# Router logits of a mixture-of-experts layer computed as two 64-column products, and one ScalarE table load moved ahead of the experts

## The chip, the cores and the metric

The kernel runs on one core of a Trainium2 chip. The metric is the device time of one execution in microseconds (us). Five engines run their own instruction streams and meet on semaphores: TensorE (matrix products), VectorE, ScalarE, GpSimd and SyncE (here it only issues transfers).

## The reference, cut to what matters

Two decoder layers over 512 tokens of width 1024; each has a mixer and then a hierarchical mixture of experts. What the change touches is the router and the start of the experts:

```python
def hierarchical_moe(h, wc, bc, wf, bf, w_gate_up, w_down):
    ...
    coarse_prob = jax.nn.softmax((xt @ wc + bc).astype(jnp.float32), axis=-1)   # 4 groups
    g_prob, g_idx = lax.top_k(coarse_prob, 1)
    fine_logits = (xt @ wf + bf).astype(jnp.float32).reshape(n, N_GROUPS, EXPERTS_PER_GROUP)
    ...
    e_logit, e_idx = lax.top_k(fine_sel, TOP_K_INNER)
    e_w = jax.nn.softmax(e_logit, axis=-1) * g_prob
    ...
    gate, up = jnp.split(gu, 2, axis=-1)
    act = jax.nn.silu(gate) * up * gates.astype(h.dtype)[..., None]
    return jnp.einsum('nef,efd->nd', act, w_down).reshape(b, t, d)
```

The kernel joins wc and wf into one matrix of 20 columns per layer.

## The kernel before

**Tiles.** The 512 tokens are 4 tiles of 128 (T = 0 to 3). TensorE computes `out = stationary^T @ moving`: the stationary operand is loaded by an LDWEIGHTS record, the moving one streamed by a MATMUL record. Dense products split each fp32 operand into a rounded high and a low part and are three products (L650, L651, L652, in helper `mm3`). The logits are plain fp32 products: one `mm` call shows as two LDWEIGHTS and two MATMUL records (64 calls over both layers, 128 records of L2023).

**The end of a mixer.** `outnorm(l, db)` on TensorE finishes the output projection tile by tile (`finish`, L650 to L652), turns the new x over (`rawT`, L1999, four transposes) and computes the logits of tiles whose halves are turned (`logits`, L2023): stationary is a 128x128 block of the turned x, moving is a 128x20 block of the router matrix, summed over eight blocks k. TensorE takes its instructions in the order written: finish(0), finish(1), rawT(0), finish(2), logits(0), rawT(1), half of finish(3), logits(1), rawT(2), the other half of finish(3), the first half of logits(3) and all of logits(2), rawT(3), the second half of logits(3). The eight calls of logits(0) are 16 records, likewise logits(1); then come 24 records in one burst, and 8 at the end.

VectorE adds each finished tile into x (L1429), copies the last turned tile out of the accumulator memory (L1451), multiplies it by the norm weight (L1452), and then runs `route(l)`, from L1736 on: some 35 small instructions in one chain that choose group and experts and build one-hot matrices. TensorE counts positions with them (L2399 to L2391); VectorE makes the rows of each expert's slots (L1780); GpSimd gathers the first two experts' tokens (L846). TensorE meanwhile multiplies for no result (`warm`, L2383), then turns the gathered tokens (L2377) and starts the experts: per expert 24 x 3 matrix products (L650 to L652), two transposes (L2447) of the activated values, and the down projection.

**ScalarE.** In `moe(l)` it takes two exponentials for the gates' weights (L1200, L1202; L1200 brings the table of Exp), then waits for the turned tokens (L1278), rounds weights (`hi`, L978 and L1227), and computes silu of the first expert's gate (L1207), which brings the table of Silu. VectorE multiplies silu by up and by the gate (L1841), behind making the low part of a weight piece (`lo`, L1836), in its own order. Copies work with whichever table is in place.

**Transfers.** SyncE streams the expert weights. Pieces from the thirteenth of a layer on wait until the first two experts' tokens have been gathered.

The logits lie in two banks of the accumulator memory, 40 columns of each: `logits_at = ps[:, 0:2, 0:40].rearrange("p b (t c) -> p t b c", t=2)`. `half(n)` is the partitions 64n to 64n+63; CH is 64, P is 128, KD is 8. `onec` is a column of ones. `A(...)` issues on ScalarE and waits for that instruction's end.

Of the kernel before, what the change touches and what calls it, by code (L numbers as in the profile page):

```python
# [26 lines left out]
ACT = mybir.ActivationFunctionType  # L27
AX = mybir.AxisListType

P = 128  # L30
# [3 lines left out]
KD = DM // P  # L34
NH = 4
DK = 128
CH = 64
# [282 lines left out]
def build(nc, a, out):  # L320
    ctx = ExitStack()
    with ctx:
        def sb(name, shape, dt=F32):
            return ctx.enter_context(nc.sbuf_tensor(name, shape, dt))

        def sem(name):
            return ctx.enter_context(nc.semaphore(name))
# [17 lines left out]
        small = sb("small", [P, 420])  # L345
# [14 lines left out]
        def reg(off, n):  # L360
            return ar[:, off:off + n]
# [5 lines left out]
        def v3(ap, k):  # L367
            return ap.rearrange("p (k n) -> p k n", k=k)
# [6 lines left out]
        onec = small[:, 412:413]  # L375
# [72 lines left out]
        def half(n):  # L448

            return slice(64 * n, 64 * n + 64)  # L450
# [25 lines left out]
        hTf = v3(reg(0, 4096), 8)  # L476
# [15 lines left out]
        def s_(name):  # L492
            if name not in SEM:
                SEM[name] = sem(name)
            return SEM[name]
# [149 lines left out]
        def cols(T, w=P):  # L645
            return slice(T * w, T * w + w)
# [43 lines left out]
        rw = v3(reg(RO + 1206, 160), 8)  # L690
# [10 lines left out]
        logits_at = ps[:, 0:2, 0:40].rearrange("p b (t c) -> p t b c", t=2)  # L701
# [267 lines left out]
        def _(act):  # L969
            A = Line(act, "act")  # L970
# [72 lines left out]
            def load_wb(n):  # L1043
                act.dma_start(wb(n), NORM_W[n].rearrange("(a n) -> a n", a=1).broadcast_to([P, DM])).then_inc(s_("wb_loaded"), 16)
# [151 lines left out]
            def moe(l):  # L1196
                m = MOE_PIECE[l]

                act.wait_ge(s_("r_cexp"), l + 1)
                A(act.activation(r_a, cd, ACT.Exp), s_("r_exp"))  # L1200
                act.wait_ge(s_("r_eexp"), l + 1)
                A(act.activation(ed, ed, ACT.Exp), s_("r_exp"))  # L1202
                used = s_("moe_used")

                def silu(E, par, count):
                    act.wait_ge(used, count)
                    act.activation(sg[:, par, :], ps[:, par, 0:FE], ACT.Silu).then_inc(s_("silu_done"), 1)  # L1207

                xT_hi(l, 0, 0)
                hi(m + 4)  # L1210
                hi(m + 5)
                xT_hi(l, 1, 1)
                hi(m + 6)
                silu(16 * l, 0, 6 * NE * l + 4)
                load_wb(2 * l + 2)

                def expert(it, par):
                    E = it * 2 + (16 * l + par)
                    b = m + 4 + 6 * par
                    last = isinstance(it, int) and it == NE // 2 - 1  # L1220

                    def hi_in(j):

                        n = b + j
                        act.wait_ge(raw_loaded[RAW_SLOTS[in_turn(n, it)]], raw_loaded_at(n, it))
                        act.wait_ge(used, it * 12 + (6 * NE * l + n - m - NSPL + 1))
                        act.activation(wh[:, n % NSPL, :, :], raw_at(in_turn(n, it)), ACT.Copy).then_inc(hi_done, 1)  # L1227

                    act.wait_ge(s_("aT_ready"), E + 1)
                    act.activation(HTH[:, 4 + par, 0:256], ps[:, 6, 0:256], ACT.Copy).then_inc(s_("aT_hi"), 1)  # L1230
                    n0 = 0
                    if not last or par == 0:
                        n0 = 4
                        for j in (3, 4, 5, 6):
                            hi_in(j)
                        silu(E + 1, 1 - par, it * 12 + (6 * NE * l + 6 * par + 8))
                        if not last:
                            xT_hi(l, it * 2 + (par + 2), par)
                        hi_in(7)
                    act.wait_ge(s_("ysb_free"), E + 1)  # L1240
                    for hf in range(2):
                        act.wait_ge(used, it * 12 + (6 * NE * l + 6 * par + 4 + n0 + hf + 1))
                        act.activation(ysb[:, par, 512 * hf:512 * hf + 512], ps[:, 2 + hf, :], ACT.Copy).then_inc(s_("y_read"), 1)
                        if hf == 0 and not last:
                            hi_in(8)

                for n in range(4):
                    expert(*divmod(n, 2))
                with act.Fori(2, NE // 2 - 1) as it:
                    for par in range(2):  # L1250
                        expert(it, par)
                for par in range(2):
                    expert(NE // 2 - 1, par)
                for i in range(4):
                    hi(m + 6 * NE + i)
                n = overflow_flag(act, l)
                with act.If(n > 0):
                    with act.Fori(0, 7) as j:
                        for g in range(2):
                            act.wait_ge(s_(f"ov_xT{l}"), j * 2 + (g + 1))  # L1260
                            act.activation(hTf[:, 4 * g:4 * g + 4, 0:P], v3(ps[:, 4 + g, :], 4), ACT.Copy).then_inc(s_(f"ov_xTr{l}"), 1)
                        act.wait_ge(s_(f"ov_gu{l}"), j + 1)
                        act.activation(sg[:, 0, :], ps[:, 0, 0:FE], ACT.Silu).then_inc(s_(f"ov_silu{l}"), 1)
                        act.wait_ge(s_(f"ov_aT{l}"), j + 1)
                        act.activation(hTf[:, 0:2, P:2 * P], ps[:, 6, 0:256].rearrange("p (k n) -> p k n", k=2), ACT.Copy).then_inc(s_(f"ov_aTr{l}"), 1)
                        for hf in range(2):
                            act.wait_ge(s_(f"ov_yp{l}"), j * 2 + (hf + 1))
                            act.activation(ysb[:, 0, 512 * hf:512 * hf + 512], ps[:, 2 + hf, :], ACT.Copy).then_inc(s_(f"ov_y{l}"), 1)

                act.wait_ge(s_("y_all_stored"), l + 1)  # L1270
                src = y2_dram[l].rearrange("(T p j) d -> T p j d", p=P, j=2)
                for T in range(NT):
                    act.dma_start(YP[:, T, :, :], src[T]).then_inc(s_(f"yp_loaded{T}"), 16)
# [8 lines left out]
            for step in SCHEDULE:  # L1282
                k = step[0]
# [674 lines left out]
        def _(pe):  # L1958
            mm = nc.tensor.matmul
# [42 lines left out]
            def outnorm(l, db):  # L2002
                def finish(t, kps=(2, 3)):
                    for kp in kps:
                        i = first_piece(db) + kp
                        if t == 0:
                            pe.wait_ge(hi_done, i + 1)
                            wait_lo(pe, i)
                        for k2 in range(2):
                            k = 2 * kp + k2  # L2010
                            ins = mm3(ps[:, t, :], HTH[:, k, cols(t)], HTL[:, k, cols(t)], wh[:, i % NSPL, k2, :], wl[:, i % NSPL, k2, :],
                                      False, k == KD - 1)
                        if t == NT - 1 and kp == 2:
                            ins.then_inc(piece_used, 1)
                    if kp == 3:
                        ins.then_inc(dense_ready, 1)

                def logits(T, halves_of_row=(0, 1)):
                    for hf in halves_of_row:
                        if hf == 1:  # L2020
                            tile_is_read(pe, ("xT", l, 1, T))
                        for k in range(4 * hf, 4 * hf + 4):
                            ins = mm(logits_at[:, T // 2, T % 2, :], hTf[:, k, cols(T)], rw[:, k, :], start=k == 0, stop=k == KD - 1)  # L2023
                    if T == NT - 1 and halves_of_row[-1] == 1:
                        ins.then_inc(s_("r_logits"), 1)

                finish(0)
                finish(1)
                rawT(l, 1, 0)
                finish(2)  # L2030
                tile_is_read(pe, ("xT", l, 0, NT - 1))
                pe.wait_ge(s_("norm_w_applied"), 2 * l + 1)
                logits(0)
                rawT(l, 1, 1)
                finish(3, (2,))
                logits(1)
                rawT(l, 1, 2)
                finish(3, (3,))
                logits(3, (0,))
                logits(2)  # L2040
                rawT(l, 1, 3)
                logits(3, (1,))
# [455 lines left out]
            for hf in range(2):  # L2498
                ins = mm(ps[:, hf, :], one_row, wrow[:, 512 * hf:512 * hf + 512], start=True, stop=True)
            ins.then_inc(s_("wb0_spread"), 1)  # L2500
            for step in SCHEDULE:
                k = step[0]
# [118 lines left out]
```

## Time and profile before

| what | value |
|---|---|
| median of 3 runs | 1235.07 us (1231.03, 1235.31, 1235.07) |
| the profiled execution, its own time | 1230.59 us |
| its span in the profile | 1228.5 us |
| TensorE busy with products | 1115.8 us, 91% of the span |
| VectorE busy | 684.2 us, 56% |
| ScalarE busy | 597.0 us, 49% |
| GpSimd busy | 421.9 us, 34% |

All stages and durations below are of the profiled execution, whose time is its span and 2.1 us around it. Layer 0's router lies at about 397 to 427 us, layer 1's at about 1011 to 1041 us. In the rows, PE is TensorE's products, PEld its weight loads, DVE VectorE, ACT ScalarE, POOL GpSimd, SP SyncE.

### The profile page before, as it was taken

The page shows a single profiled execution, that of the slowest core. Times are in us where ns is not written, and L with a number is a line of the kernel's source. Part 1 is how long each engine was busy: PE and PEld are TensorE (multiplying, and loading weights), DVE is VectorE, ACT ScalarE, POOL GpSimd, SP SyncE. Part 2 cuts the span into 40 slices and gives each one's busy share as a digit, 9 for nine tenths or more (in the row PEclk, how much of TensorE's full clock was granted, in tenths as well). Part 3 has the DMA queues.
Part 4 walks back from the last instruction along what each step waited for, and adds up shares of the span by engine and source line. Part 5 has one row for each costly group of instructions (what it writes and reads, how often), then busy time and mean ns, then how long its engine had stood idle before and what let it go on. Part 6 is the DMA issues. An engine that isn't in the chain of part 4 may idle for free.

```text
span 1228.5 us, 19674 instructions
## 1 busy us (share of the span) xinstructions
PE 1115.8 (91%) x7081; PEld 918.3 (75%) x7081; DVE 684.2 (56%) x973; ACT 597.0 (49%) x873; POOL 421.9 (34%) x350
## 2 busy tenths in 40 slices
PE   6998999999979799998399999999999997999980
PEld 4786888778758578886378888888888885788870
DVE  3434424358633699997614532542433136999975
ACT  4546233251423389998232324333253233899871
POOL 4342311210205134444434243542434431344442
PEclk8999999999989799999599999999999997999995
DMA  9232211102206399997633232232212262999955
GB/s 250 57 86 52 54 53 36 53 32 74 69 1 201 114 362 371 378 375 257 242 96 102 78 94 70 86 105 76 94 63 93 86 197 98 359 375 366 365 205 214
DMA packets 89285, 194.75 MB, mean 159 GB/s; under 512 B 20158, under 2 KB 21242, under 8 KB 88187
## 3 DMA queue, kind: packets, MB, share of 16 engines
q1 hardware_dynamic: 67562, 159.87, 39.0%
q10 hardware_dynamic: 11856, 17.07, 4.0%
q0 software_dynamic: 9792, 16.80, 3.7%
q8 instruction: 49, 0.80, 0.3%
q14 instruction: 26, 0.21, 0.1%
HBM read 189.50 MB, written 23.07 MB: 173 GB/s over the span
## 4 chain that ended last, share of the span: by engine, by line
PE 82%; DVE 8%; ACT 3%; DMA 3%; issue 2%; SPq 1%; POOL 1%; POOLq 0%; DVEq 0%; ACTq 0%
PE ps L650 23%; PE ps L651 22%; PE ps L652 22%; PE ps L2377 2%; PE ps L2169 2%; DMA raw<-in_moe_w_down_dram 1%; PE ps L2023 1%; PE ps L2383 1%; DMA arena<-y 1%; PE ps L2307 1%; PE ps L2055 1%; DVE arena L1410 1%; DVE x L1391 1%; DVE x L1392 1%; DMA x<-in_x_dram 1%
## 5 line engine op out<-in xcount | busy, mean ns | idle before, releaser
L814 POOL TENSOR_TENSOR wl<-raw,wh 128x1024 fp32r<-128x1024 f32 x100 | 243.1, 2439 | 423.1 <-ACT wh L978 422.7
L650 PE MATMUL ps<-wh,hT_hi 128*128 128x512 f32 x864 | 349.7, 405 | 13.3 <-DVE hT_lo L1461 6.0
L652 PE MATMUL ps<-wh,hT_lo 128*128 128x512 f32 x864 | 340.0, 393 | 0.0
L651 PE MATMUL ps<-wl,hT_hi 128*128 128x512 f32 x864 | 339.8, 393 | 0.0
L978 ACT ACTIVATE wh<-raw 128x1024 fp32r<-128x1024 f32 x116 | 122.7, 1068 | 221.9 <-PE ps L652 203.2
L650 PEld LDWEIGHTS ps<-wh,hT_hi 128*128 128x128 f32 x864 | 164.3, 190 | 49.2 <-DVE hT_lo L1461 6.9
L652 PEld LDWEIGHTS ps<-wh,hT_lo 128*128 128x128 f32 x864 | 163.9, 190 | 35.2
L651 PEld LDWEIGHTS ps<-wl,hT_hi 128*128 128x128 f32 x864 | 164.4, 190 | 31.2
L650 PE MATMUL ps<-hT_hi,wh 128*128 128x512 f32 x288 | 117.4, 407 | 8.2 <-ACT arena L1136 5.3
L1836 DVE TENSOR_TENSOR wl<-arena,wh 128x1024 fp32r<-128x1024 f32 x96 | 114.0, 1222 | 5.5 <-ACT wh L1227 3.9
L1836 DVE TENSOR_TENSOR wl<-raw,wh 128x1024 fp32r<-128x1024 f32 x92 | 109.5, 1224 | 11.6 <-ACT wh L978 4.8
L651 PE MATMUL ps<-hT_lo,wh 128*128 128x512 f32 x288 | 114.8, 399 | 0.0
L652 PE MATMUL ps<-hT_hi,wl 128*128 128x512 f32 x288 | 114.3, 397 | 0.0
L1227 ACT ACTIVATE wh<-arena 128x1024 fp32r<-128x1024 f32 x94 | 98.8, 1070 | 8.9 <-PE ps L652 6.1
L1227 ACT ACTIVATE wh<-raw 128x1024 fp32r<-128x1024 f32 x84 | 88.1, 1072 | 7.3 <-PE ps L652 3.3
L650 PEld LDWEIGHTS ps<-hT_hi,wh 128*128 128x128 f32 x288 | 55.4, 192 | 22.8 <-issue 4.3
L652 PEld LDWEIGHTS ps<-hT_hi,wl 128*128 128x128 f32 x288 | 55.6, 193 | 12.1
L651 PEld LDWEIGHTS ps<-hT_lo,wh 128*128 128x128 f32 x288 | 55.7, 193 | 11.0
L859 POOL COPY cur_rows<-slot_rows 128x1 uint32 (+1 forms) x32 | 8.5, 267 | 134.7 <-PE ps L2377 134.7
L825 POOL TENSOR_TENSOR small<-small 128x4 f32<-128x4 f32 (+1 forms) x10 | 13.9, 1394 | 100.7 <-DVE small L1580 100.7
L992 ACT ACTIVATE arena<-x 128x1024 f32<-128x1024 f32 x20 | 21.2, 1058 | 52.1 <-DVE x L1392 36.8
L1278 ACT ACTIVATE hT_hi<-ps 128x512 fp32r<-128x512 f32 x64 | 34.7, 595 | 20.3 <-PE ps L2377 18.9
(317 smaller groups left out, 1561.8 us busy)
## 6 DMA issues: line engine op xcount, KB each, us to landing
raw<-in_moe_w_gate_up_dram SPq DMA_DIRECT2D x64, 512.0 KB
arena<-in_moe_w_gate_up_dram SPq DMA_DIRECT2D x64, 512.0 KB, 6.7
raw<-in_odd_w_in_dram SPq DMA_DIRECT2D x48, 512.0 KB
raw<-in_even_w_in_dram SPq DMA_DIRECT2D x32, 512.0 KB
arena<-in_moe_w_down_dram SPq DMA_DIRECT2D x32, 512.0 KB, 7.8
raw<-in_moe_w_down_dram SPq DMA_DIRECT2D x32, 512.0 KB
arena<-y ACTq DMA_DIRECT2D x8, 1024.0 KB, 8.2
raw<-in_odd_w_out_dram SPq DMA_DIRECT2D x16, 512.0 KB
```

What stands on the lines that cost most here:

```text
L650: nc.tensor.matmul(dst, lh, rh, start=first, stop=False)
L651: nc.tensor.matmul(dst, lh, rl, start=False, stop=False)
L652: return nc.tensor.matmul(dst, ll, rh, start=False, stop=last)
L814: pool.tensor_tensor(columns_of(i, wl[:, i % NSPL, :, :]), raw_columns(i), columns_of(i, wh[:, i % NSPL, :, :]).bitcast(F32), ALU.subtract ...
L825: pool.tensor_tensor(dst, src, mhalf[:, 0:n], ALU.pow).then_inc(on, 1)
L978: act.activation(columns_of(i, wh[:, i % NSPL, :, :]), raw_columns(i), ACT.Copy).then_inc(hi_done, 1)
L992: A(act.activation(squares(n), X[:, T, :], ACT.Square, scale=DM ** -0.5, accum_out=ss[:, T:T + 1]), s_("norm_ss"))
L1227: act.activation(wh[:, n % NSPL, :, :], raw_at(in_turn(n, it)), ACT.Copy).then_inc(hi_done, 1)
L1278: act.activation(HTH[:, 2 * par + g, :], ps[:, 4 + g, :], ACT.Copy).then_inc(s_("xT_hi"), 1)
L1836: tt(wl[:, n % NSPL, :, :], raw_at(in_turn(n, it)), wh[:, n % NSPL, :, :].bitcast(F32), ALU.subtract).then_inc(lo_dve, 1)
L2169: blocks(name, lambda o, b, n: mm(o, of_block(lh, b, n), of_block(rh, b, n), start=True, stop=True))
L2377: ins = tr(ps[:, 4 + g, cols(j)], xg[:, par, 4 * g + j:DM:KD], ident[:, :])
```

## The change

The logits of a tile are computed as two products of 64 tokens each, one into the upper and one into the lower 64 partitions of the same accumulator columns, alternating inside each k. And `moe(l)` gets one more ScalarE instruction behind the second exponential: silu of one value per partition into an unused column of `small`.

```diff
                 A(act.activation(r_a, cd, ACT.Exp), s_("r_exp"))
                 act.wait_ge(s_("r_eexp"), l + 1)
                 A(act.activation(ed, ed, ACT.Exp), s_("r_exp"))
+                A(act.activation(small[:, 413:414], onec, ACT.Silu))
                 used = s_("moe_used")
...
                         for k in range(4 * hf, 4 * hf + 4):
-                            ins = mm(logits_at[:, T // 2, T % 2, :], hTf[:, k, cols(T)], rw[:, k, :], start=k == 0, stop=k == KD - 1)
+                            for n in range(2):
+                                o = P * T + CH * n
+                                ins = mm(logits_at[half(n), T // 2, T % 2, :], hTf[:, k, o:o + CH], rw[:, k, :], start=k == 0, stop=k == KD - 1)
                     if T == NT - 1 and halves_of_row[-1] == 1:
                         ins.then_inc(s_("r_logits"), 1)
```

## Rows read from the trace of the kernel before

**Rows 1.** The page: the chain that ended last, by line.

```profile
PE ps L650 23%; PE ps L651 22%; PE ps L652 22%; PE ps L2377 2%; PE ps L2169 2%; DMA raw<-in_moe_w_down_dram 1%; PE ps L2023 1%; PE ps L2383 1%; DMA arena<-y 1%; PE ps L2307 1%; PE ps L2055 1%; DVE arena L1410 1%; DVE x L1391 1%; DVE x L1392 1%; DMA x<-in_x_dram 1%
```

**Rows 2.** Stretches: length, busy us and records of engines, TensorE clock, DMA share, GB/s.

```profile
397.00:410.00 13.00, 12.15 (x92) 11.14 (x90) 5.87 (x7) 3.56 (x7) 2.38 (x6) 1.00 0.46 185
...
440.00:480.00 40.00, 40.00 (x201) 33.65 (x200) 38.89 (x43) 36.56 (x52) 17.20 (x24) 1.00 0.96 364
```

**Rows 3.** Timeline, layer 0, TensorE: start, length, instruction, idle time before it.

```profile
397.50 0.40 PE L652 MATMUL ps<-wh,hT_lo 128*128 128x512 f32 x1
...
397.73 1.86 PE L2023 MATMUL ps<-arena 128*128 128x20 f32 x16
...
399.44 0.63 PE L1999 MATMUL ps<-ident,x 128*128 128x128 f32 x4
...
404.85 2.75 PE L2023 MATMUL ps<-arena 128*128 128x20 f32 x24
...
407.44 0.64 PE L1999 MATMUL ps<-ident,x 128*128 128x128 f32 x4
```

**Rows 4.** Timeline, layer 0, the hand-over from the logits to the router.

```profile
405.12 0.69 DVE L1429 TENSOR_TENSOR x<-x,ps 128x512 f32<-128x512 f32 x1 [2.90 <-PE ps L652]
...
408.18 0.69 DVE L1451 COPY arena<-ps 128x512 f32<-128x512 f32 x1 [2.38 <-PE ps L1999]
408.91 1.22 DVE L1452 TENSOR_TENSOR arena<-x,arena 128x1024 f32<-128x1024 f32 x1
...
410.17 0.24 DVE L1736 TENSOR_TENSOR arena<-ps,small 128x80 f32<-128x80 f32 x1
```

**Rows 5.** Timeline, layer 1, the same hand-over.

```profile
1022.33 1.22 DVE L1452 TENSOR_TENSOR arena<-x,arena 128x1024 f32<-128x1024 f32 x1
1022.35 1.90 PE L2023 MATMUL ps<-arena 128*128 128x20 f32 x8 [0.85 <-DVE arena L1451]
...
1024.38 0.24 DVE L1736 TENSOR_TENSOR arena<-ps,small 128x80 f32<-128x80 f32 x1 [0.83 <-PE ps L2023]
```

**Rows 6.** Timeline, TensorE, a burst of 32 records with 64-column stationary blocks.

```profile
124.19 0.39 PE L652 MATMUL ps<-hT_hi,wl 128*128 128x512 f32 x1
124.51 1.15 PE L2182 MATMUL ps<-arena 128*64 128x64 f32 x32
125.59 0.50 PE L650 MATMUL ps<-hT_hi,wh 128*128 128x512 f32 x1
125.93 0.40 PE L651 MATMUL ps<-hT_lo,wh 128*128 128x512 f32 x1
```

**Rows 7.** Timeline, TensorE, a burst of 64 such records, and what follows it.

```profile
288.07 2.06 PE L2307 MATMUL ps<-arena 128*64 128x32 f32 x64
290.06 0.50 PE L650 MATMUL ps<-wh,hT_hi 128*128 128x512 f32 x1
```

**Rows 8.** Timeline, layer 0, the first expert's gate.

```profile
433.27 0.39 PE L652 MATMUL ps<-wh,hT_lo 128*128 128x512 f32 x1
433.48 1.28 ACT L1207 ACT_TABLE_LOAD   x1
...
433.54 1.21 DVE L1836 TENSOR_TENSOR wl<-arena,wh 128x1024 fp32r<-128x1024 f32 x1
...
435.19 0.42 DVE L1841 TENSOR_TENSOR arena<-arena,ps 128x256 f32<-128x256 f32 x1 [0.43 <-ACT arena L1207]
```

**Rows 9.** Timeline, layer 0, ScalarE between the second exponential and its next work.

```profile
415.36 0.20 ACT L1202 ACTIVATE arena<-arena 128x4 f32<-128x4 f32 x1
...
425.03 1.09 ACT L1278 ACTIVATE hT_hi<-ps 128x512 fp32r<-128x512 f32 x2 [9.47 <-PE ps L2377]
```

**Rows 10.** Stretches around layer 1's last logits, columns as in rows 2.

```profile
1006.00:1021.00 15.00, 15.00 (x103) 13.59 (x102) 5.99 (x7) 6.39 (x11) 3.73 (x9) 1.00 0.31 128
1021.00:1025.00 4.00, 2.39 (x12) 1.94 (x10) 2.47 (x5) 1.15 (x1) 0.30 (x1) 0.52 0.32 131
```

**Rows 11.** SyncE's wait before the stream of a layer's expert weights.

```profile
SPq L748 <- DMA arena<-hs,slot_rows: 33.9, 1, 33.9
```

## The prediction

> **What bounds the kernel now.** Start with the page's chain that ended last [rows 1]: the three dense-product lines alone are 67% of it, and the logits' line L2023 is 1%, some 12 us over two layers. So the change can only work on a small part, and its worth has to be read from the stretch where that part lies. The stretches show that TensorE works 12.15 of 13.00 us around the logits of layer 0 [rows 2]: what shortens TensorE's order there moves everything behind it. The timeline of the stretch says what ends it: VectorE's L1429 idles for a product, L1451 idles for the last transposes (L1999), L1452 follows, and the router's L1736 starts only when L1452 is through [rows 4]. From L1736 on, VectorE's chain sets the time, not TensorE. In layer 1 the last wait is another one: L1452 ends at 1022.33 + 1.22 = 1023.55, and L1736 waits 0.83 us more for the last eight logits records [rows 5].
>
> **Part one: the logits in halves.** A call shows as two records, so the 16 records of a tile become 32, the burst of 24 becomes 48 and the last 8 become 16. The work per record is what I must price from elsewhere, since no 64-column logits are in this trace.
>
> Before: from the start of a 16-record burst to the start of the transposes behind it is 399.44 - 397.73 = 1.71 us, and 407.44 - 404.85 = 2.59 for the 24 [rows 3]: 0.107 us a record. That is not the streaming of 20 columns; it is the pace at which full 128-column blocks are loaded and used.
>
> After: the nearest rows are bursts that alternate between the lower and the upper 64 output partitions, as the change does, with 64 or 32 moving columns. From burst start to the next product's start, 32 records take 125.59 - 124.51 = 1.08 us [rows 6] and 64 take 290.06 - 288.07 = 1.99 [rows 7]. The difference, 0.91 us for 32 records, is 0.028 a record, and 1.08 - 0.91 = 0.17 is a fixed part. Entering and leaving costs more: the burst begins 0.32 us behind the product before it, the full-width logits begin 0.23 behind theirs (397.50 to 397.73) [rows 3], which adds 0.09. The first product after the burst takes 0.34 to the next one (125.59 to 125.93), 0.11 over that pace; full-width bursts lose something behind them too, so I count 0.03 of it, a choice, and keep the other 0.08 for the range. So I take 0.12 for the change of shape beside the 0.17 in the burst.
>
> - A 16-record burst: 1.08 + 0.12 = 1.20 in place of 1.71, a gain of 0.51. There are two before the last finish, 1.02.
> - The burst of 24: 1.08 + 16 x 0.028 + 0.12 = 1.65 in place of 2.59, a gain of 0.94.
> - The last 8: 8 x 0.107 = 0.86 becomes 1.08 - 16 x 0.028 = 0.63 plus 0.12, a gain of 0.11. In layer 0 it is worth nothing: it begins with L1452 and is over before L1452 ends after 1.22 us, and would be up to 0.1 without that cover.
>
> Does something else become late before the transposes? Tile 3's x must be added first: L1429 takes 0.69 us from 405.12 [rows 4], and moves 1.02 earlier with the last finish, to 404.10 to 404.79. TensorE would be ready for the last transposes at 407.44 - 1.96 = 405.48. TensorE still decides, by 0.7 us. So L1451, L1452 and L1736 all come 1.02 + 0.94 = 1.96 us earlier in layer 0.
>
> In layer 1 the same 1.96 us come off, and the extra wait of 0.83 can go too. There TensorE's granted clock was 1.00 from 1006 to 1021 and 0.52 on average from 1021 to 1025 [rows 10], that is mostly the 1.2 GHz level; the last eight records took 1.90 us in place of some 0.86 to 1.1. TensorE had gone through the 24-record burst just before the clock fell. At the lower level, with everything doubled, the 16 half-width records would take about 1.26 + 0.12 = 1.38 us, 0.2 past L1452; at the upper one they hide wholly. Bounds of this term: 0 (other executions may not have the fall there) and 0.83. I take 0.7, nearer to the row of this execution.
>
> Behind L1736 the whole train moves: the router's chain, the gather, the warm-up products, the experts. The weight stream is the thing that might stay behind, for in the experts' stage DMA is at 0.96 of its share and 364 GB/s [rows 2]. But SyncE waited 33.9 us for the gathered tokens before it went on with the stream [rows 11], so the stream starts earlier with the router. GpSimd has nothing in its queue before that gather that the change would touch.
>
> A rule speaks against the halves. The nearest rows change shape twice at a price of 0.09 to 0.12 us, already in the sum. The Trainium skill says in "TensorEngine Tiling (Array Packing)", Key Properties, that a change of tiling mode drains TensorE; it names no price, so by that rule too each of the eight bursts pays, and the sum stays as the rows make it; the trace agrees, with 0.32 us in place of 0.23 at the entrance [rows 6].
>
> **Part two: the table.** The new instruction adds one table load (1.28 us, the duration of L1207's own [rows 8]) and one small activation (0.20, as L1202) on ScalarE, behind 415.56. ScalarE then sat idle 9.47 us before L1278 [rows 9], so these 1.48 us are hidden; without that cover they would be on the path, 1.5 us a layer. Queued behind it are only the roundings of the turned tokens, which wait for TensorE anyway. The exponentials have signalled before it, so nobody else waits.
>
> At the other end L1207's load goes. It started at 433.48, and the last product of the gate began at 433.27 and took 0.39, to 433.66. So silu could start at about 433.7 in place of 434.77, ending at 434.1. But L1841, which uses it, stands behind L1836 on VectorE, which ends at 433.54 + 1.21 = 434.75 [rows 8]. Before, L1841 started at 435.19 after 0.43 idle. What is late next is thus L1836, and of 1.28 us only 0.43 come off. TensorE's next instructions in its order are the transposes of L1841's result, so the 0.43 are on the path, in layer 1 likewise (its table load has the same place there).
>
> **The sum.** Layer 0: 1.96 + 0.43 = 2.4. Layer 1: 1.96 + 0.7 + 0.43 = 3.1. Together 5.5 us off the profiled execution's 1230.59, giving 1225.1; off the median of 1235.07, 1229.6. The four executions known are 1230.59, 1231.03, 1235.07 and 1235.31: two levels some 4 us apart, equally often. The median happens to be of the upper pair, so a new median may fall in either. Between 1225.1 and 1229.6, leaning to the upper value, I forecast **1228.5 us**.
>
> **Rivals.**
>
> *The halves do not overlap (0.10).* Two 64-column blocks might cost what one of 128 does: 0.053 us a record. Then 32 records take 1.71 + 0.12, a loss of 0.12 a burst, 0.36 a layer before the router, and only the table's 0.86 remains: 1235.07 - 0.86 + 0.72 = 1234.9. The Trainium skill gives such a rule, in "TensorE: Matmul & The Clock Gate", Part 3, The mechanism: weight loads overlap with products in flight only when the row group differs; here it does not. Against this rival: the bursts of rows 6 and 7 have all 128 rows too, alternate in columns alone, and ran at 0.028.
>
> *Accumulation makes half-width records slow (0.05), slower than before.* The logits sum eight k into the same 20 columns; rows 6 and 7 do not sum over calls. If each record waited for its forerunner in the accumulator and kept the 0.107, 56 more records ahead of the last transposes would cost 6.0 us a layer, and the last burst 16 x 0.107 = 1.71 would outlast L1452 by 0.5. Both layers: 13.0 + 0.5 for shape changes - 0.86 = 12.6 more, 1247.7. It decides against the change from (1.71 - 0.29) / 32 = 0.044 us a record. Against it: the two records of one call already go to the same place in rows 6 and 7, and full-width logits run at the same 0.107 whatever they sum.
>
> *Gained, and given back (0.13).* The experts' stage runs into the weight stream, at 0.96 of DMA, or the clock rises later against the first experts' products, since the fall and rise need not move with the work. One layer's part of 2 to 3 us is lost: 1235.07 - 2.5 = 1232.6. For it: the two levels of the runs show that something of 4 us varies. Against it: the stream starts with the gather [rows 11].
>
> *My forecast (0.72).* Its own range is 1224 to 1231.5: sums from 4.8 (no clock term) to 5.6, each from either level, and a microsecond for the price of a shape change before transposes, which no row shows.
>
> **How the numbers follow.** A measurement of this kernel tells about 0.5% from nothing, that is 6.2 us: below 1228.9 is faster. The forecast's 0.72 splits by the level of the median: 0.50 faster, 0.22 the same. The given-back rival adds 0.03 faster and 0.10 same; no overlap adds 0.08 same and 0.02 slower; accumulation 0.05 slower. Faster 0.53, same 0.40, slower 0.07. The range 1223 to 1233 takes in the forecast's own and the given-back case, and leaves out the two others with 0.15.
>
> **What the profile after would show.** L2023 in 256 records at 128x64 blocks, each 16-record place at 1.1 us and the long one at 1.6; last transposes some 2 us nearer to the stretch's start; L1736 directly behind L1452 in both layers; a table load behind L1202 and none at L1207, with L1841 directly behind L1836. The prediction is wrong if the records come at over 0.04 us, if TensorE idles for L1429 or L1016's copies inside the bursts, if the gather does not move with L1780, or if TensorE waits in the experts where it did not before.

## The result, and the profile after

The changed kernel takes 1223.59 us (median of 6 runs, 1220.57 to 1227.23) against 1230.59 us for the kernel before in 6 runs (1229.73 to 1235.31): the ratio is 0.9939, with a 95% interval of 0.9917 to 0.9960. That is 7.0 us off by the medians, 7.5 by the ratio, with an interval of 4.9 to 10.2. The profiled execution took 1223.59 us, its span is 1221.4 us against 1228.5.

The kernel's line numbers move: L1451 of before is L1452 here, L1736 is L1737, L1841 is L1842, L1999 is L2000, L2023 is L2026, L2377 is L2380, L1207 is L1208.

The chain that ended last, from the page of the changed kernel. The logits, 1% of the chain before [rows 1], are no longer in what it lists:

```profile
span 1221.4 us, 19932 instructions
...
PE ps L650 23%; PE ps L652 22%; PE ps L651 22%; PE ps L2380 2%; PE ps L2172 2%; DMA raw<-in_moe_w_gate_up_dram 1%; DMA arena<-y 1%; DVE arena L1411 1%; PE ps L2310 1%; ACTq L1346 1%; PE ps L2058 1%; DVE x L1392 1%; DVE x L1393 1%; PE ps L2386 1%; PE ps L2135 1%
```

The bursts of layer 0 in the timeline of the changed kernel, to be read against [rows 3]:

```profile
396.17 1.11 PE L2026 MATMUL ps<-arena 128*64 128x20 f32 x32
...
397.22 0.66 PE L2000 MATMUL ps<-ident,x 128*128 128x128 f32 x4
...
401.89 0.39 PE L652 MATMUL ps<-wh,hT_lo 128*128 128x512 f32 x1
402.21 1.58 PE L2026 MATMUL ps<-arena 128*64 128x20 f32 x48
```

From the burst's start to the transposes it is 1.05 us in place of 1.71, and 1.51 (402.21 to 403.72) in place of 2.59. Entering costs 0.32 behind the product before it, 0.09 more than full width. A 32-record burst thus gains 0.57 and the long one 0.99, 2.13 us a layer.

The hand-over to the router in layer 0, and the same in layer 1, against [rows 4, 5]:

```profile
405.20 1.22 DVE L1453 TENSOR_TENSOR arena<-x,arena 128x1024 f32<-128x1024 f32 x1
405.23 0.65 PE L2026 MATMUL ps<-arena 128*64 128x20 f32 x16 [0.85 <-DVE arena L1452]
406.46 0.24 DVE L1737 TENSOR_TENSOR arena<-ps,small 128x80 f32<-128x80 f32 x1
...
1017.50 1.22 DVE L1453 TENSOR_TENSOR arena<-x,arena 128x1024 f32<-128x1024 f32 x1
1017.52 0.65 PE L2026 MATMUL ps<-arena 128*64 128x20 f32 x16 [0.85 <-DVE arena L1452]
1018.76 0.24 DVE L1737 TENSOR_TENSOR arena<-ps,small 128x80 f32<-128x80 f32 x1
```

In both layers the router now starts directly behind L1453. Layer 1's wait of 0.83 us is gone: the last logits took 0.65 us in place of 1.90. The two are not at the same clock: in the kernel before it had fallen to 0.50 when they ran, here it was still at 1.00 (from 1017.5 to 1018.2 us). At 1.00 the full-width ones took 1.07 us, in layer 0 of the kernel before, and caused no wait either.

The table, in the timeline of the changed kernel, against [rows 8, 9]. The load sits behind the second exponential; silu (L1208) starts as soon as its product is there; and the gate's product (L1842) now stands directly behind the weight piece (L1837):

```profile
411.65 0.20 ACT L1202 ACTIVATE arena<-arena 128x4 f32<-128x4 f32 x1
411.87 1.28 ACT L1203 ACT_TABLE_LOAD   x1
...
421.18 1.09 ACT L1279 ACTIVATE hT_hi<-ps 128x512 fp32r<-128x512 f32 x2 [7.81 <-PE ps L2380]
...
429.81 1.22 DVE L1837 TENSOR_TENSOR wl<-arena,wh 128x1024 fp32r<-128x1024 f32 x1
429.97 0.38 ACT L1208 ACTIVATE arena<-ps 128x256 f32<-128x256 f32 x1 [0.24 <-PE ps L652]
430.94 0.42 DVE L1842 TENSOR_TENSOR arena<-arena,ps 128x256 f32<-128x256 f32 x1
431.50 0.43 PE L2450 MATMUL ps<-ident,arena 128*128 128x128 f32 x2 [1.35 <-DVE arena L1842]
```

**Where the 7.1 us of the span came from.** The starts of the same instructions in the two profiles, and how far the changed kernel is ahead:

| place | before | after | ahead | gained since |
|---|---|---|---|---|
| layer 0, first logits | 397.73 | 396.17 | 1.56 | 1.56 |
| layer 0, router (L1736, L1737) | 410.17 | 406.46 | 3.71 | 2.15 |
| layer 0, first gate's product | 435.19 | 430.94 | 4.25 | 0.54 |
| layer 1, first logits | 1011.05 | 1008.47 | 2.58 | -1.67 |
| layer 1, router | 1024.38 | 1018.76 | 5.62 | 3.04 |
| end of the span | 1228.5 | 1221.4 | 7.1 | 1.5 |

The changed code cannot reach the first row's 1.56 us: they lie ahead of it. The changed kernel was 0.8 us ahead at 12 us of the span and 1.6 at 30, behind a stretch (12 to 30 us) whose clock was 0.72 before and 1.00 after. The 2.15, 0.54 and 3.04 lie where the change works, though 0.89 of the 3.04 also hangs on where the clock fell. Of the last row's 1.5, 0.5 is layer 1's share of the table load. The loss of 1.67 and the other 1.0 are the odd ones, and lie in the experts' stages. There TensorE goes from expert to expert in 9.35 us, until it meets late weights. (In the trace an expert is 12 x 3 products of L650 to L652, 8 x 3 for gate and up and 4 x 3 for down, not the 24 x 3 named ahead.) Waits among the changed kernel's experts, two of ScalarE's from 540 to 575 us and then one of TensorE's from 430 to 600 us (waiting line, awaited, us in total, times, longest):

```profile
ACT wh L1228 <- DMA raw<-in_moe_w_gate_up_dram: 1.6, 1, 1.6
ACT wh L1228 <- DMA arena<-in_moe_w_gate_up_dram: 1.4, 2, 1.0
```

```profile
PE ps L650 <- DVE hT_lo L1829: 1.1, 2, 0.9
```

In layer 0 the kernel before had only 0.2 us of ScalarE waiting for weights there, and no such wait of TensorE; it lost 2.0 us in layer 1. What this is, and why the moved load did more than the 0.43 us foretold for it, is what the experiments are about.

### The profile page after: what moved, and what is told of

It is laid out like the page before. It is cut to its first block, busy times and chain, and to the rows that moved or that the text cites. A ratio compares the mean times of both kernels' runs of the same rounds, so it can differ in the third digit from the quotient of the medians.

```text
span 1221.4 us, 19932 instructions
## 1 busy us (share of the span) xinstructions
PE 1109.1 (91%) x7209; PEld 909.9 (74%) x7209; DVE 687.5 (56%) x973; ACT 597.0 (49%) x875; POOL 423.2 (35%) x350
## 4 chain that ended last, share of the span: by engine, by line
PE 80%; DVE 9%; DMA 3%; ACT 3%; issue 2%; ACTq 1%; SPq 1%; POOL 1%; POOLq 0%; DVEq 0%
PE ps L650 23%; PE ps L652 22%; PE ps L651 22%; PE ps L2380 2%; PE ps L2172 2%; DMA raw<-in_moe_w_gate_up_dram 1%; DMA arena<-y 1%; DVE arena L1411 1%; PE ps L2310 1%; ACTq L1346 1%; PE ps L2058 1%; DVE x L1392 1%; DVE x L1393 1%; PE ps L2386 1%; PE ps L2135 1%
## 5 line engine op out<-in xcount | busy, mean ns | idle before, releaser
L650 PE MATMUL ps<-wh,hT_hi 128*128 128x512 f32 x864 | 349.0, 404 | 13.3 <-DVE hT_lo L1462 6.1
L652 PE MATMUL ps<-wh,hT_lo 128*128 128x512 f32 x864 | 339.9, 393 | 0.0
L650 PEld LDWEIGHTS ps<-wh,hT_hi 128*128 128x128 f32 x864 | 164.1, 190 | 49.4 <-DVE hT_lo L1462 7.0
L652 PEld LDWEIGHTS ps<-wh,hT_lo 128*128 128x128 f32 x864 | 163.5, 189 | 35.0
L650 PE MATMUL ps<-hT_hi,wh 128*128 128x512 f32 x288 | 117.5, 408 | 7.0 <-ACT arena L1136 4.1
L1837 DVE TENSOR_TENSOR wl<-arena,wh 128x1024 fp32r<-128x1024 f32 x96 | 114.0, 1223 | 5.4 <-ACT wh L1228 4.1
L1837 DVE TENSOR_TENSOR wl<-raw,wh 128x1024 fp32r<-128x1024 f32 x92 | 109.7, 1224 | 11.9 <-ACT wh L1228 5.1
L652 PE MATMUL ps<-hT_hi,wl 128*128 128x512 f32 x288 | 114.7, 398 | 0.0
L650 PEld LDWEIGHTS ps<-hT_hi,wh 128*128 128x128 f32 x288 | 55.7, 193 | 22.0 <-issue 4.3
L652 PEld LDWEIGHTS ps<-hT_hi,wl 128*128 128x128 f32 x288 | 55.6, 193 | 12.1
```

The lines of the kernel that those rows point to most:

```text
L650: nc.tensor.matmul(dst, lh, rh, start=first, stop=False)
L652: return nc.tensor.matmul(dst, ll, rh, start=False, stop=last)
L1837: tt(wl[:, n % NSPL, :, :], raw_at(in_turn(n, it)), wh[:, n % NSPL, :, :].bitcast(F32), ALU.subtract).then_inc(lo_dve, 1)
```

## The experiments

Each ran beside the kernel before on the same chip. The theories: (1) the halves give most, since the two halves' records overlap; (2) the moved load gives more than it takes off the path. The main rival to the second is that it gives just that. All times in us.

| kernel | median (runs) | ratio to before, 95% interval |
|---|---|---|
| changed kernel | 1223.59 (6) | 0.9939, 0.9917 to 0.9960 |
| e1 halves, load not moved | 1226.20 (7) | 0.9961, 0.9945 to 0.9976 |
| e2 load moved, full width | 1228.68 (12) | 0.9979, 0.9968 to 0.9990 |
| e3 halves in turn | 1225.48 (9) | 0.9962, 0.9948 to 0.9976 |
| e4 quarters | 1221.56 (4) | 0.9920, 0.9897 to 0.9943 |
| e5 halves, load not moved, gap filled | 1223.60 (6) | 0.9950, 0.9935 to 0.9965 |
| e6 a lighter weight stream | 1220.64 (4) | 0.9917, 0.9903 to 0.9931 |
| e7 gate's product first | 1223.41 (6) | 0.9939, 0.9925 to 0.9953 |
| e8 quarters, gate's product first | 1221.40 (6) | 0.9924, 0.9910 to 0.9938 |
| e9 before, gap filled | 1229.19 (12) | 0.9990, 0.9978 to 1.0002 |
| e11 quarters, gap filled | 1222.14 (6) | 0.9926, 0.9911 to 0.9941 |

The kernel before itself had medians of 1230.86 (23 runs, 1227.38 to 1233.34), 1231.01 (11) and 1230.91 (17, to 1235.03) beside them. e10 and e12 are single runs.

### e1: the halves alone, and e2: the moved load alone

```diff
 # e1
-                A(act.activation(small[:, 413:414], onec, ACT.Silu))
 # e2
-                            for n in range(2):
-                                o = P * T + CH * n
-                                ins = mm(logits_at[half(n), ...], hTf[:, k, o:o + CH], ...)
+                            ins = mm(logits_at[:, T // 2, T % 2, :], hTf[:, k, cols(T)], ...)
```

> The halves without the moved table load. Theory (most of the gain comes from the halves): the bursts of L2026 as in the changed kernel (1.1 us for 32 records, 1.6 for 48), the first gate's table load back at its old place with about 0.5 us more TensorE idle per layer; 5 to 6.5 us faster than before, that is 0.995 to 0.996 of its time. Rival (the table load is what gave most): under 2 us faster.

> The moved table load with the logits in full width. Theory: TensorE's gap before the first activated values' transposes shrinks from 2.0 to 1.5 us in each layer, so about 1.0 us faster than before, 0.999 of its time. Rival (a ScalarE load of 1.28 us off the path in each layer): 2.6 us faster, 0.998.

Measured: 1226.2 for the halves, 4.8 us off by the ratio, a little under the range; 1228.7 for the load, 2.6 off by the ratio, where 1.0 was expected. TensorE's gap shrank as said in e2, from 2.03 to 1.51 us between product starts in both layers. So the size matches the rival's, but not its mechanism. The trace of e1 has the answer. Its table load is at the old place, and here is what followed the gap in layer 0, in stretches (length, busy us and records of PE, PEld, DVE, ACT, POOL, then the granted clock, DMA share, GB/s):

```profile
431.00:434.00 3.00, 1.14 (x14) 0.68 (x13) 2.50 (x7) 2.12 (x3) 0.32 (x1) 1.00 1.03 379
434.00:435.00 1.00, 1.00 (x5) 0.81 (x4) 0.86 (x5) 0.79 (x2) 0.00 (x0) 0.79 1.04 422
435.00:436.00 1.00, 1.00 (x4) 0.77 (x3) 0.83 (x6) 0.54 (x1) 0.00 (x0) 0.50 1.01 406
436.00:438.00 2.00, 2.00 (x6) 1.54 (x5) 1.93 (x5) 1.06 (x1) 0.00 (x0) 0.50 1.03 390
```

TensorE was busy 1.14 of 3 us, and then, though busy all the time, at the 1.2 GHz level (0.50). The first products of the second expert took 0.63 us each in place of 0.39. The same in layer 1 of e1:

```profile
1049.00:1053.00 4.00, 4.00 (x12) 0.58 0.99 377
```

The same stretch of the changed kernel's layer 0, whose gap was 0.5 us shorter, stayed at 2.4 GHz:

```profile
432.00:436.00 4.00, 4.00 (x18) 3.29 (x18) 3.66 (x13) 3.43 (x4) 0.00 (x0) 1.00 1.02 379
```

The price can be read from the starts of the gate's product from expert to expert. Intervals of the first four experts:

```
changed kernel, layer 0      8.04  8.89  9.35
e1, layer 0                  9.19  9.35  9.35
e1, layer 1                  9.18  9.37  9.34
```

That is 1.6 us lost a layer. In this execution of e1 the load at its old place cost 0.5 + 1.6 us in each layer.

### e5: fill the gap instead of moving the load, and e9: fill it in the kernel before

```diff
                 slots_to_rows(over_at, hotO, ...).then_inc(s_("r_rows"), 1)
+                warm(6)     # six 128x512 products for no result
```

> The halves without the moved table load, and TensorE multiplies six more times for no result in the two idle microseconds ahead of the first activated values' transposes (1.4 of the 2.0 us filled). Theory (the 2.0 us of idle are followed by a stretch at the 1.2 GHz level, which costs the first experts about 1.6 us a layer; the moved load helps most by shortening that gap): no lower clock between the first and the third expert in either layer, and 2 to 3.5 us less than with the halves alone, that is 1223 to 1224.5. Rival (the moved load is worth what it takes off the path, 0.5 us a layer): the time of the halves alone, 1226, since the gap itself stays.

> The kernel before with the six filling products ahead of the first activated values' transposes, nothing else changed. Theory (the kernel before meets the 1.2 GHz level after its gap of 2.0 us in some executions and layers, which is why the moved load alone gained 2.2 us and not the 0.9 to 1.0 that it takes off the path): no lower clock there, and 1 to 2 us less than before, 1229 to 1230. Rival (the kernel before keeps its clock there always, as in its profile, and the moved load's 2.2 us have another source): within 0.5 us of before.

Measured: e5 has a median of 1223.60, inside its range, with the table load still on ScalarE's path. Its timeline shows the filling products (L2385) between the last group and the transposes, and a clock of 1.00 behind them in both layers:

```profile
430.62 1.62 PE L2385 MATMUL ps<-hT_hi 128*128 128x512 f32 x6
432.63 0.43 PE L2450 MATMUL ps<-ident,arena 128*128 128x128 f32 x2 [0.39 <-DVE arena L1841]
```

```profile
430.00:440.00 10.00, 9.61 (x55) 1.00 1.02 398
1040.00:1050.00 10.00, 9.61 (x55) 1.00 1.02 367
```

The median is that of the changed kernel, but the ratios put e5 between the two: 6.2 us off, against 4.8 for e1 and 7.5 for the changed kernel. That is what the account asks for, since the filling prevents the fall (1.6 us an execution on average, see below) and leaves the load's 2 x 0.5 us on the path. The ratios' intervals overlap, so this is carried by the trace (the intervals between gates are 8.05 and 8.85 us in e5), not by the timing alone. e9 came out at 1229.19, 1.2 us under before by the ratio and 1.7 by the medians, within its expectation, but with an interval that just reaches 1: this run by itself does not prove it. The 1.6 us expected on average lie within that interval.

### e10 and e12: how often does the clock fall there?

No edit: the kernel before, and e1, once more.

> The kernel before once more, for a second profile. Theory: either a stretch at 1.2 GHz behind the gap in at least one layer and second and third experts that are 0.5 to 1.1 us longer there, or the state of the first profile; a TensorE wait at experts 12 to 15 in one layer or both.

> The halves without the moved load once more, for a second profile. Theory (the fall behind the 2.0 us gap depends on where the gap lies in the chip's own time): the 1.2 GHz level follows the gap in none, one or both layers, and wherever it does, the first two intervals between experts' gates are 9.2 and 9.35 us, and elsewhere 8.05 and 8.9.

Measured: e10 took 1230.93 us and had the fall in layer 0, not in layer 1; e12 took 1225.64, and had it in layer 0 and not in layer 1, too. The stretches behind the gap, of e10 and then e12:

```profile
436.00:439.00 3.00, 3.00 (x9) 0.51 1.02 397
```

```profile
434.00:437.00 3.00, 3.00 (x8) 0.50 1.01 395
...
1035.00:1050.00 15.00, 12.44 (x69) 1.00 0.85 311
```

The intervals agree: 9.16 and 9.35 us in e10's layer 0 against 8.04 and 8.88 in its layer 1; 9.21 and 9.37 against 8.05 and 8.88 in e12. Over all profiles: with the gap of 2.0 us (before, e10, e1, e12) the lower clock followed in 4 of 8 layers. With the load moved (changed kernel, e2, e3, e4, e6, e7, e8, e11) in none of 16: ten of these with the gap of 1.5 us, four with 1.0 (e7, e8), two with it filled (e11). With the gap filled in the old place (e5, e9) it followed in none of 4. Four of eight is a rough share, and the cause of its coming and going is not shown. At one in two, moving the load saves 2 x 0.5 for the path and about 2 x 0.8 on average for the clock, 2.6 us. That is e2's 2.6, and the 2.6 between the medians of e1 and the changed kernel.

The profiles show a second fall that comes and goes: the one ahead of a layer's last eight logits records. Where the clock was 1.00 during them (layer 0 of before, layer 1 of e2), the router waited 0.03 to 0.04 us; at 0.63 (layer 0 of e10) 0.48; at 0.50 (the other five layers of the four profiles at full width) 0.82 to 0.83. With halves (changed kernel, e1, e3, e5, e6, e7, e12) the router waited in none of 14 layers. In most of them the fall came only after the burst, so that they do not test a burst at the lower clock. The nearest to a test is layer 1 of e5, where the mean clock was 0.55 over the 16 records:

```profile
1016.21 1.22 DVE L1452 TENSOR_TENSOR arena<-x,arena 128x1024 f32<-128x1024 f32 x1
1016.23 1.00 PE L2025 MATMUL ps<-arena 128*64 128x20 f32 x16 [0.85 <-DVE arena L1451]
...
1017.47 0.24 DVE L1736 TENSOR_TENSOR arena<-ps,small 128x80 f32<-128x80 f32 x1
```

They took 1.00 us and were still hidden behind L1452's 1.22.

### e3: halves in turn, and e4: quarters

```diff
 # e3: eight records of one half, then eight of the other
-                        for k in range(4 * hf, 4 * hf + 4):
-                            for n in range(2):
+                        for n in range(2):
+                            for k in range(4 * hf, 4 * hf + 4):
 # e4: four blocks of 32 tokens
-                            for n in range(2):
-                                o = P * T + CH * n
-                                ins = mm(logits_at[half(n), T // 2, T % 2, :], hTf[:, k, o:o + CH], ...)
+                            for n in range(4):
+                                o = P * T + 32 * n
+                                ins = mm(logits_at[32 * n:32 * n + 32, T // 2, T % 2, :], hTf[:, k, o:o + 32], ...)
```

> The same 64-column products, but four k of the lower half and then four k of the upper one, so that eight records in a row have the same half. Theory (what makes the halves cheap is that the weight load of one half runs beside the product in the other): the pace falls to about 0.053 us a record, 32 records take 1.8 to 2.0 us, as much as full width or more, and the gain on the whole shrinks to 0 to 2 us. Rival (a narrower block is cheaper by itself, whatever its neighbour is): 0.028 a record as in the changed kernel, and its whole gain of 7 us.

> The logits as four products of 32 tokens each, alternating over the four quarters. Theory (a record cannot be had under about 0.028 us, so that halves are the best width): a tile's 64 records take about 2.0 us, more than the 1.7 us of full width, and the burst of 96 about 2.9; the gain on the whole is gone, 1 to 3 us slower than before without the table's share. Rival (the pace is set by the columns loaded, so quarters take 0.014 us a record): a tile's 64 records take 1.1 us, the same time as the changed kernel or up to 0.3 us less a burst.

The first burst of e3's layer 0 and the transposes behind it:

```profile
397.10 1.42 PE L2026 MATMUL ps<-arena 128*64 128x20 f32 x32
398.45 0.65 PE L2000 MATMUL ps<-ident,x 128*128 128x128 f32 x4
```

1.35 us, between the changed kernel's 1.05 and full width's 1.71: neither 1.8 to 2.0 nor the rival's 1.05. The single records say why. In the changed kernel they start alternately 7 and 51 ns apart, a pair in 58: the two halves go side by side. (A record does not name its half; that is inferred from the program's order and from e3.) In e3 records with the same half before and behind them start 58 ns apart. But where one group of eight meets the next, most come 26 to 32 ns apart and one pair 6, closer than records of one half ever come alone. So the next half's records must have started beside the former's. The load records have the same rhythm (6 or 7 and 49 to 52 ns in the changed kernel), so loads of both halves run side by side too; whether load or product sets the 58 ns is not separated. So both statements of the theory hold for single records (a half by itself costs 58 ns, and the gain comes from the neighbour being the other half), and the sum made of them was wrong, since part of the overlap came about by itself. The whole took 1225.48, 1.9 more than the changed kernel, the 1.9 us that the slower bursts make over both layers (2 x 0.30 and 0.36 in each); the two ratios' intervals overlap, so the agreement is closer than the timing can show.

The first and the long burst of e4's layer 0, and their transposes:

```profile
395.13 0.74 PE L2026 MATMUL ps<-arena 128*32 128x20 f32 x64
395.81 0.66 PE L2000 MATMUL ps<-ident,x 128*128 128x128 f32 x4
...
400.43 1.01 PE L2026 MATMUL ps<-arena 128*32 128x20 f32 x96
401.43 0.63 PE L2000 MATMUL ps<-ident,x 128*128 128x128 f32 x4
```

64 records in 0.68 us, 96 in 1.00: 0.010 us a record. My theory of a floor of 0.028 a record is wrong. The rival was right that quarters are cheaper still, and with its 0.014 too careful. The kernel is 1221.56, 2.0 under the changed one, though the intervals of the two ratios overlap. Part of the bursts' 1.2 us a layer isn't had: the router now waits for something else, the last tile's scale from GpSimd. VectorE in layer 0 of e4:

```profile
402.89 1.23 DVE L1453 TENSOR_TENSOR arena<-x,arena 128x1024 f32<-128x1024 f32 x1
404.63 0.24 DVE L1737 TENSOR_TENSOR arena<-ps,small 128x80 f32<-128x80 f32 x1 [0.52 <-POOL small L830]
```

### e6: a lighter weight stream

From the thirteenth weight piece of a layer on, each piece that goes to one of the six plain buffers is loaded for half its columns; the experts' results use old values there.

```diff
-                sp.dma_start(raw_at(i), piece_src(i))...
+                dst, src = raw_at(i), piece_src(i)
+                if RAW_SLOTS[i] < NRAW and any(m + 12 <= i < m + 6 * NE for m in MOE_PIECE):
+                    dst, src = dst[:, :, 0:256], src[:, :, 0:256]
+                sp.dma_start(dst, src)...        # likewise in the loop
```

> The changed kernel, with every weight piece that goes to one of the six plain buffers loaded for half its columns only, from the thirteenth piece of a layer on, so that a quarter less is streamed in the experts' stage (the output uses old values in the other half). Theory (part of the gain in layer 0 was given back at experts 12 to 14, where TensorE ran into the weight stream): no TensorE wait there in either layer, an expert every 9.35 us from the third to the last, and 2 to 4 us less than the changed kernel, about 1220.5. Rival (what was lost there comes from something other than the stream, such as the gathers or GpSimd's order): the waits stay, and the time within 1 us of 1223.6.

Measured: 1220.64, 3.0 under the changed kernel, with another result of the computation. The same stretch of the late experts, first of the changed kernel, then of e6 (PE busy, clock, DMA share, GB/s):

```profile
540.00:560.00 20.00, 18.94 (x92) 1.00 1.00 355
```

```profile
540.00:560.00 20.00, 20.00 (x101) 1.00 0.71 248
```

The intervals between the last six gates of layer 0 are 9.46, 10.51, 10.51, 8.84, 9.04 in the changed kernel from the eleventh on, and 9.35 (9.34 to 9.41) in e6. Both layers of e6 are free of them, so the waits are from the stream. Against e6, the late experts (the tenth interval on) cost the kernel before 0.0 and 2.0 us in its two layers, the changed one 1.6 and 0.6, e5 0.0 and 1.5, e9 0.4 and 0.3, e1 0.9 and 0.0, e2 1.1 and 2.8, e3 2.5 and 1.8, e4 0.9 and 3.2, e7 0.4 and 1.8, e8 1.0 and 0.7, e10 0.0 and 1.0, e11 0.2 and 0.6, e12 0.5 and 0.9. So most of the 1.67 us lost in the table of the result is this wait, and the 1.0 gained is its opposite: 2.0 - 0.6 = 1.4 us, of which 0.4 went again behind the experts. The wait fell in another layer, and the two executions lost 2.0 and 2.2 in all. In this pair of profiles it is thus not the change's gain given back. On average that is open. The three profiles with logits and load as before lost 2.0, 1.0 and 0.7 us over both layers, 1.2 on average; the ten changed ones (e6 left out) lost 0.8 to 4.3, 2.3 on average. The spread is too wide for one profile a kernel to settle it, and the kernel before was not run with the lighter stream.

### e7 and e8: the gate's product ahead of the weight piece; e11: the gap filled as well

```diff
 # e7 (and e8, on top of the quarters), VectorE
-                lo_in(m + 6)
                 gated(16 * l, 0)
+                lo_in(m + 6)
 # e11, on top of the quarters, TensorE: warm(4) where e5 has warm(6)
```

> The changed kernel with two VectorE instructions of the first expert swapped: the gate's product ahead of the low part of weight piece 6. Theory (behind the moved load VectorE's weight piece is what holds the gate): TensorE's gap there shrinks from 1.5 to about 1.0 us in both layers, and 0.5 to 1.1 us come off the whole. Rival (the weight piece made later is missed by TensorE at once): the gap moves to the products of the second expert, no change.

> Logits in quarters, the moved table load, and the swap of the run before. Theory: the two add, 2 to 2.5 us from the quarters and up to 1 us from the swap below the changed kernel, so 1220 to 1221. Rival (what the router gains is given back to the weight stream): within 1 us of the changed kernel's 1223.6.

> Quarters, the moved load, and four filling products in the 1.5 us gap. Theory (with the moved load the gap is too short for the clock to fall anyway): no change from the quarters alone, 1221 to 1222. Rival (it still falls in some executions): 0.5 to 1.5 us less and a narrower spread.

e7: 1223.41 against 1223.59, no change; the rival was right. The gap fell from 1.51 to 0.96 us between product starts, and a new one of 1.07 came behind it: TensorE at once misses the weight piece that was put back. The waits of e7's TensorE from 425 to 445 us:

```profile
PE ps L2450 <- DVE arena L1842: 0.8, 1, 0.8
PE ps L650 <- DVE wl L1837: 0.7, 1, 0.7
```

e8 is 1221.40, as the quarters alone (1221.56). It lies within its range, but the swap adds nothing to it. e11 is 1222.14, also the same: with the load moved there is no fall left for the filling to prevent. The fastest version with the whole computation is thus the quarters with the moved load, 0.8% under before, in e4; of e4, e8 and e11 none is clearly ahead of another.

## Why the prediction was right, and where it was off

- **Halves.** Right in mechanism and size. Foretold were 1.96 us a layer; 2.13 came by the bursts, 2.15 by the shift of layer 0's router. A 32-record burst gained 0.57 where 0.51 was foretold, the long one 0.99 for 0.94: the bursts of 64-column blocks [rows 6, 7] were a good measure, a little dear. Summing over k costs nothing, so the rival of slow accumulation fell with the records' pace.
- **No overlap.** That rival fell as well. The rule of "TensorE: Matmul & The Clock Gate", Part 3, The mechanism, in the Trainium skill, that weight loads overlap products in flight only when the row group differs, does not hold as far as the whole pace goes: in the changed kernel all records have all rows and differ in columns only, and a pair of different halves started every 58 ns, as did a single record between two of the same half (e3).
- **Change of shape.** 0.09 us at the entrance as foretold; what the burst costs behind it was inside the 0.17 taken.
- **The last eight records' wait.** Foretold 0.7 for layer 1's 0.83; all of it went, 3.04 - 2.15 = 0.89 us with the rest. That was counted for one layer because the one profile had it in one. At full width six of eight layers had it, 4.7 us over four executions, so the term is worth 1.2 us on average. The price of the half-width records at the lower clock, 1.38 us and 0.2 past L1452, was too high as far as e5's 1.00 us at a mean clock of 0.55 tells.
- **Table load, what it frees.** 0.43 us a layer foretold; TensorE's gap shrank by 0.51, and L1842 stood behind L1837, as said. The load at its new place cost nothing: 7.81 us of idle time were left behind it.
- **Table load, what it prevents.** This was missed. The sum took the gap of 2.0 us as a wait that costs its own length. It also lets the clock fall in one layer of two, at 1.6 us each. The profile of before did not show it, since that execution was spared in both layers.
- **Behind the router.** That all moves with it is right: the lead won in layer 0 stayed constant to 0.03 us over its first eleven experts. "TensorE waits in the experts where it did not before" was named as a sign of being wrong, and it came, 1.6 us in layer 0. It proves less than was thought, since the kernel before has such waits too, in the other layer. The rival's 1232.6 did not come; whether a part of the gain is given back on average is open (see e6).
- **The sum, and the forecast.** 5.5 us of 1230.59, 1225.1, was the sum. Two terms were too small for an average execution: nothing in place of 1.6 us for the fall behind the gap, and 0.7 in place of 1.2 for the router's wait. With both it would have been 7.6, where 7.0 was measured by the medians; the interval of 4.9 to 10.2 us holds the 5.5 as well. The 1228.5 named was 4.9 us too high. The 1223.59 lies 0.6 us inside the range of 1223 to 1233 and just below the forecast's own 1224 to 1231.5, so it was a near thing. The mechanisms held, and the step that failed is the one from the sum to the median: "two levels some 4 us apart, equally often", leaning to the upper one. The runs of the kernel before beside the experiments spread over 1227.4 to 1235.0, with medians of 1230.9 to 1231.0. They do not fall into two levels; three runs had given a high median, and a drop from the profiled execution's own time was the better forecast. That execution lay in the middle.

## What to carry to other kernels

Products with few moving columns and a 128-column stationary block can be bound by the stationary block. Here their pace went with its width, and 64-column blocks came as pairs every 58 ns with 20 moving columns as with 64. Split the columns in halves or quarters that go to different output partitions, and alternate them record by record. A gap of TensorE is to be priced by what the clock does behind it, too, and one profile may not show that: compare several, or fill the gap once as a test. A wait that one layer shows and the other does not may be just as common in both. And before a gain on the path is credited, look at the instruction that stands directly behind the freed one, in its engine's own order: here it took 0.8 of 1.28 us, and swapping the two only moved the wait.

## What the runs showed of the hardware

- Blocks of 128 rows by 32 columns, four alternating, with 20 moving columns, came every 0.010 us (e4), by 64 columns every 0.029 (58 ns a pair), by 128 columns every 0.11.
- Records of two neighbouring groups of eight that went to different halves started 6 to 32 ns apart, where records of one half come every 58 ns: the groups overlapped, though the program has one after the other (e3).
- A gap of 2.0 us between TensorE's products was followed by a stretch at 1.2 GHz, with TensorE busy throughout, in 4 of 8 layers; gaps of 1.5 us and less at that place in none of 20. Twenty such chances do not make a threshold, and a fall needs no such gap: at full width the clock was at the lower level throughout the last eight logits in 5 of 8 layers, having fallen while the transposes behind the long burst ran, or within 0.1 us of them.
